# One VectorE and one ScalarE queue reordered around the first output chunk, and one transpose round moved inside a unit

## The chip, the cores and the metric

One core of one Trainium2 chip. The metric is device microseconds of one execution. The kernel before took 497.25 us, the median of 3 runs (497.24 to 497.35).

## The reference

One layer of a model that mixes two kinds of attention, for 256 tokens of width 2048, in float32:

```
h    = rmsnorm(x, g_norm)
proj = h @ w_in                       # 2048 -> 7704 columns: q, k, v, z of both kinds, gates
y_moba = rmsnorm(moba_attention(rope(m_q), rope(m_k), m_v) * silu(m_z), g_out_moba)
y_nsa  = rmsnorm(nsa_attention(rope(n_q), n_q, compressed, selected and window k, v, gates)
                 * silu(n_z), g_out_nsa)
x    = x + concatenate([y_moba, y_nsa]) @ w_out
out  = rmsnorm(x, g_final)
```

The compressed keys of the second kind come from a small two-layer network (`w_ck1`, `w_ck2` and, for the values, `w_cv1`, `w_cv2`), and its raw queries meet these compressed keys without rotation.

## The kernel before

Tokens are two row blocks of 128 (`m` = 0, 1). The input projection is cut into 15 column chunks of 512 (`CHUNKS`), the output projection into 4 more (chunks 15 to 18, `NC` = 15, called output chunk 0 to 3). A **unit** is the part of a chunk that comes from 512 rows of the weight (4 blocks of 128). Units are numbered in the order in which their weights are loaded. Four of them are spoken of often:

- unit 54 is group 1 of output chunk 1 (`UNIT_NO[NC + 1, 1]`)
- units 55, 56 and 57 are groups 1, 2 and 3 of output chunk 0 (`UNIT_NO[NC, 1]` and so on)

To keep float32 precision each operand is split in a rounded part and a residual (`w_hi`, `w_lo`, `xT_hi`, `xT_lo`), and each product is three matmuls (`three_products`, L754 to L756): hi by hi, lo by hi, hi by lo. A unit is 2 row blocks x 4 blocks x 3 = 24 matmuls of 128x512. Its weights go this way:

- SP loads 1 MB into one of three `w_raw` buffers. The load of unit u waits until VectorE has split unit u - 3 (L514).
- ScalarE rounds it into `w_hi` (`hi`, L1189). It waits for the load, and for the ring of three `w_hi`/`w_lo` slots: `unit_used` must count the user of the slot three places back.
- VectorE writes the residual into `w_lo` (`lo`, L1567).
- TensorE waits for `lo_ready` and multiplies.

Five pairs of chunks (`PAIRS`) compute four of their blocks by seven products in place of eight (P1 to P7, `seven`). The pair of output chunks 0 and 1 is called `OA`. It has its own order: `oa_first` (P1, P5, then unit 54), `oa_second` (P2, P6, row block 0 of unit 55, P7, P3), `oa_third` (row block 1 of unit 55, P4). Its weight blocks are rounded by ScalarE (`block_hi`, L1257) and VectorE (`block_lo`, L1850); four intermediate results are copied out of PSUM by ScalarE (`mid_out_`, L1273) and added to the result by DMAs that GpSimd issues (L719). Row block 1 of unit 55 waits for the fourth copy.

The attention result `y` is scaled (`y_scale`), transposed on TensorE (`y_round_`, L735, eight rounds numbered 0 to 7), multiplied by its gain on VectorE (`y_times_g`, L1897), rounded by ScalarE (`y_hi`, L1402) and its residual taken by VectorE (`y_residual`, L1907). Rounds 0 to 3 are the first half of `y`; rounds 4 and 5 are read by unit 56 (`ylo_done` at 6), rounds 6 and 7 by unit 57 (`ylo_done` at 8). `ys` is a combination of parts of `y` for P5 and others, rounded by `ys_round` (L1244) and `ys_residual` (L1824). The last gate chunk z is evacuated by `scaled` on VectorE (L1783), goes through Silu on ScalarE (L1288) and is multiplied into `xo` by GpSimd (L703).

Time is laid out in **slots**. Every engine runs the same loop over slots, and in each slot the `if` lines say which helper is called and in which order. There is no scheduler: what stands first in this code is first in the engine's queue, and a wait in it holds all that stands behind it. `ROUNDED_AT` says in which slot which unit is rounded. `OA_SLOT` is 60, so slots 60 to 62 hold `oa_first` to `oa_third`, slot 63 unit 56 and slot 64 unit 57. `ROUNDS` says after which slots projected rows are transposed on TensorE (`round_`). Round 16 and round 17 transpose the two row blocks of the first four raw queries of the gated (NSA) attention; ScalarE copies each out of the one bank `b_t` into `Q` (`round_out`, L1315) and issues two DMAs from it. Slot 17 runs unit 16. After it, in slot 18, TensorE runs the second layer of the compression network (L997) and the scores of the compressed keys (`cmp_scores`, L1046), which wait for both rounds' copies.

Of the kernel before, what the change touches and what calls it, by code (L numbers as in the profile page):

```python
# [47 lines left out]
NC = len(CHUNKS)  # L48
# [64 lines left out]
UNIT_NO = {u: n for n, u in enumerate(UNITS)}  # L113
# [11 lines left out]
def unit_at(slot):  # L125

    for p, (a, b) in enumerate(X_PAIRS):
        s0 = MIDDLE[p]
        if s0 <= slot < s0 + 2 * UPC:
            return {2: UNIT_NO[a, 2], 3: UNIT_NO[a, 3], 4: UNIT_NO[b, 1], 5: UNIT_NO[b, 2], 7: UNIT_NO[b, 3]}.get(slot - s0)  # L130
    a, b = PAIRS[OUT_PAIR]
    late = LATE[OUT_PAIR]
    if slot >= MIDDLE[OUT_PAIR]:
        return {late + 1: UNIT_NO[a, 2], late + 2: UNIT_NO[a, 3], late + 3: UNIT_NO[b, 1]}.get(slot)
    if slot >= OA_SLOT:
        return UNIT_NO[NC + OUT_UNITS[slot - OA_SLOT - 3][0], OUT_UNITS[slot - OA_SLOT - 3][1]] if slot > OA_SLOT + 2 else None
    return UNIT_NO[slot // UPC, slot % UPC]
# [2 lines left out]

ROUNDED_AT = {9: 10, 10: 11, 11: 12, 12: 13, 13: 14, 14: 15, 15: 16, 17: 17,
              41: 40, 42: 41, 43: 42, 44: 43, 45: 44, 46: 45, 47: 46, 49: 47, 50: 48, 52: 49, 53: 50, 54: 51, 55: 52, 56: 53,
              62: 56, 63: 58, 65: 59, 66: 60, 67: 61, 68: 62, 69: 63, 70: 64, 71: 65}


def rounded_at(slot):
# [42 lines left out]
Q_RAW, Q_MQ, Q_MK = 0, [8, 0], [12, 4]  # L189
Q_COS, Q_SIN = 8, 9  # L190
TRIG_SLOT = 14

def transpose_rounds():
    out = {}
    for i, (kind, _, n) in enumerate(CHUNKS):
# [7 lines left out]
        elif kind in ("mq", "mk"):  # L205
            out[s], out[s + 1] = (kind, (n, 0), i), (kind, (n, 1), i)
    out[TRIG_SLOT] = ("trig", 0, 0)
    return out


ROUNDS = transpose_rounds()
# [83 lines left out]
def build_layer(nc, x, positions, inv_freq, w_in, g_norm, pe_ck, pe_cv, w_ck1, w_ck2, w_cv1, w_cv2,  # L295
# [4 lines left out]
    with ExitStack() as ctx:  # L300
# [431 lines left out]
        def _(pe):  # L732
# [72 lines left out]
                    last = first_product(u, kind, m, k)  # L805
                last.then_inc(unit_used, 1)

            def unit(u):
                if u < UPC:
                    return first_unit(u)  # L810
                c, g = UNITS[u]
                if c >= NC:
                    pe.wait_ge(ylo_done, 4 if g < 2 else 2 * g + 2)
                if g == 0:
                    bank_free(c)
                if u == UPC:
                    pe.wait_ge(xg_early, 2 * UK)
                pe.wait_ge(lo_ready, u - FIRST + 1)
                for m in range(MT):
                    for k in range(UK):  # L820
                        last = three_products(*operands(u, m, k), g == 0 and k == 0, g == UPC - 1 and k == UK - 1, c in PAIR_OF)
                last.then_inc(unit_used, 1)
# [309 lines left out]
            for slot in range(LAST):  # L1132
                for p in range(len(PAIRS)):
                    if slot == EARLY[p] and p != OUT_PAIR:
                        pair_early(p)
                    if slot == MIDDLE[p]:
                        pair_middle(p)
                    if slot == LATE[p]:
                        pair_late(p)
                if slot == OA_SLOT:  # L1140
                    oa_first()
                if slot == OA_SLOT + 1:
                    oa_second()
                if slot == OA_SLOT + 2:
                    oa_third()
                if unit_at(slot) is not None:
                    unit(unit_at(slot))
                if slot == EARLY[OUT_PAIR]:
                    pair_early(OUT_PAIR)
                if slot == 2:  # L1150
                    pe.wait_ge(crow_in, 64)
                    pe.wait_ge(xg_early, 2 * UK)
                    nc.tensor.transpose(b_s[:, 0:P], crows, ident[:, :]).then_inc(crows_T, 1)
                if slot in ROUNDS:
                    round_(slot)
                for c in range(8):
                    if CK_SLOT[c] == slot:
                        ck_unit(c)
                if slot in CK_SUM_SLOT:
                    ck_quarters(CK_SUM_SLOT.index(slot))  # L1160
                if slot in CK2_SLOT:
                    ck_layer2(CK2_SLOT.index(slot))
                if slot in CMP_TOKEN_SLOT:
                    cmp_token(CMP_TOKEN_SLOT.index(slot))
                if slot in CMP_T_SLOT:
                    cmp_T(CMP_T_SLOT.index(slot))
                if slot in CMP_SCORE_SLOT:
                    cmp_scores(CMP_SCORE_SLOT.index(slot))
                if slot == GATE_SLOT:
                    gates()  # L1170
                if slot == GATE_SLOT + 1:
                    gate_quarters()
                if slot - 3 in JOB_AT and ends_head(JOB_AT[slot - 3]):
                    values(JOB_AT[slot - 3])
                if slot - 2 in JOB_AT:
                    prob_T(JOB_AT[slot - 2])
                if slot in JOB_AT:
                    scores(JOB_AT[slot])
                for r in Y_ROUNDS.get(slot, []):
                    y_round_(r)  # L1180
# [3 lines left out]
        def _(act):  # L1184
# [74 lines left out]
            def mid_out_(p, i):  # L1259

                if i == 1:
                    act.wait_ge(unit_used, RING_NO["early", p] + 1)
                else:
                    act.wait_ge(mid_done, 3 * p + (1, 0, 2, 3)[i])
                if p == Z1 and i == 0:
                    act.wait_ge(t_round, len(ROUNDS))
                if p == Z2 and i == 0:
                    act.wait_ge(pv_done, 2 * NH)
                if p == Z2 and i in (1, 2):
                    act.wait_ge(y_done, 2)  # L1270
                if p == OA:
                    act.wait_ge(y_done, 6)
                    nc.scalar.activation(mid_copy(p, i), mid_bank(p, i)[:, :], ACT.Copy, scale=-1.0 if i else 1.0).then_inc(mid_out, 1)  # L1273
                    return
                if p == OUT_PAIR:
                    act.wait_ge(y_done, 8)
                    act.wait_ge(oa_added, 64)
                    nc.scalar.activation(mid_copy(p, i), mid_bank(p, i)[:, :], ACT.Copy).then_inc(mid_out, 1)
                    return
                m = (0, 1, 0, 1)[i]  # L1280
                nc.scalar.activation(mid_copy(p, i), mid_bank(p, i)[:, :], ACT.Copy, scale=rstd[:, m:m + 1]).then_inc(mid_out, 1)
# [143 lines left out]
            for slot in range(NSLOT):  # L1425
# [11 lines left out]
                if slot == OA_SLOT:  # L1437
                    block_hi(OA, 3)
                    y_hi(Y_ROUNDS[57][0])
                    mid_out_(OA, 0)  # L1440
                    mid_out_(OA, 1)
                    hi(UNIT_NO[NC, 1])
                    y_squares(3)
                    block_hi(OA, 4)
                    block_hi(OA, 5)
                    mid_out_(OA, 2)
                if slot == OA_SLOT + 1:
                    mid_out_(OA, 3)
                    block_hi(OA, 6)
# [105 lines left out]
        def _(dve):  # L1555
# [8 lines left out]
            def lo(u):  # L1564
                dve.wait_ge(hi_ready, u - FIRST + 1)
                wh, wl = split_of(u)
                nc.vector.tensor_tensor(wl, w_raw[:, u % RAW], wh.bitcast(F32), ALU.subtract).then_inc(lo_ready, 1)  # L1567
# [254 lines left out]
            def ys_residual():  # L1822
                dve.wait_ge(xs_hi_ok, 3)
                nc.vector.tensor_tensor(ys_lo, ys, ys_hi.bitcast(F32), ALU.subtract).then_inc(xs_lo_ok, 1)  # L1824
# [22 lines left out]
            def block_lo(p, n):  # L1847
                dve.wait_ge(blk_hi, 7 * p + n + 1)
                hi_, lo_ = block_split(p, n)
                nc.vector.tensor_tensor(lo_, block_raw(p, n), hi_.bitcast(F32), ALU.subtract).then_inc(blk_lo, 1)  # L1850
# [20 lines left out]
            def y_scale(half):  # L1871
                dve.wait_ge(rstdy_ok, half + 1)
                for m in range(MT):
                    y = xo[:, m, half * HW:(half + 1) * HW]
                    nc.vector.tensor_scalar(y, y, rstdy[:, half, m:m + 1], None, ALU.mult).then_inc(y_scaled, 1)
# [100 lines left out]
            for slot in range(NSLOT):  # L1976
# [14 lines left out]
                if slot in (8, 40):  # L1991
                    xs_residual((8, 40).index(slot))
                if slot == 57:
                    ys_residual()
                    block_lo(OA, 0)
                    block_lo(OA, 1)
                if slot == OA_SLOT:
                    lo(UNIT_NO[NC + 1, 1])
                    y_parts(Y_ROUNDS[57])
                    block_lo(OA, 2)  # L2000
                    block_lo(OA, 3)
                    lo(UNIT_NO[NC, 1])
                    block_lo(OA, 4)
                    block_lo(OA, 5)
                    y_scale(1)
                if slot == OA_SLOT + 1:
                    block_lo(OA, 6)
                for p in range(len(PAIRS)):
# [119 lines left out]
```

## Time and profile before

| what | value |
|---|---|
| median of 3 runs | 497.25 us |
| the profiled execution, by the device's clock | 497.4 us |
| its span (first to last instruction) | 495.6 us |
| granted TensorE clock, mean over the span | 0.996 of full speed |
| TensorE matmul busy | 484.2 us, 98% of the span |
| VectorE busy | 357.7 us, 72% |
| ScalarE busy | 267.0 us, 54% |
| GpSimd busy | 76.0 us, 15% |
| DMA | 102.22 MB, mean 206 GB/s |

The profiled execution took 497.4 us for a span of 495.6 us; the 1.8 us between them lie before and after the recorded instructions. In a timeline a row is one instruction, or several merged: its start, its length, engine, line, operation, output and inputs, a count, and in brackets how long the engine had been idle before it and what released it. Matmuls overlap: one of 128x512 is recorded with 0.39 us, but the next starts 0.23 us after it, so the distance from start to start is what a matmul costs.

### The profile page before, as it was taken

To read this page: it belongs to the slowest core of one execution; us is meant where nothing else is said; L and a number is where in the kernel's file an instruction comes from. 1 tells how busy PE (TensorE), PEld (TensorE's weight loads), DVE (VectorE), ACT (ScalarE), POOL (GpSimd) and SP (SyncE) were. 2 spreads that over 40 slices of the span, in tenths; PEclk is the share of its full clock that TensorE was granted. 3 is DMA by queue.
4 is the path that set the end of the run, shared out by engine and by line. 5 is a ranking of instruction groups with operands and counts; after the bars stand their busy time and mean duration, and the time that the engine had idled before them with its cause. 6 is when DMAs were issued, how large, how long until landed. Compare 5 with 4: busy or idle time off the path is not lost.

```text
span 495.6 us, 6581 instructions
## 1 busy us (share of the span) xinstructions
PE 484.2 (98%) x2508; PEld 401.6 (81%) x2508; DVE 357.7 (72%) x568; ACT 267.0 (54%) x383; POOL 76.0 (15%) x75
## 2 busy tenths in 40 slices
PE   8999999999999999999999999999999999899994
PEld 7887787777788888888888888888888887688883
DVE  5888855932799948766587878765877787988644
ACT  5886353632656535544544464665665675466422
POOL 2340100100102202000020200000534236040220
PEclk9999999999999999999999999999999999999998
DMA  8989894577476452543443734446699948973404
GB/s 291 335 278 385 300 327 154 186 264 250 138 261 192 171 171 85 171 154 106 166 167 131 255 93 147 145 162 263 216 293 304 291 170 233 310 265 104 149 1 169
DMA packets 59311, 102.22 MB, mean 206 GB/s; under 512 B 4784, under 2 KB 15632, under 8 KB 58896
## 3 DMA queue, kind: packets, MB, share of 16 engines
q1 hardware_dynamic: 55136, 97.08, 56.6%
q0 software_dynamic: 1936, 3.67, 4.2%
q10 hardware_dynamic: 2208, 1.06, 0.9%
q8 instruction: 20, 0.33, 0.3%
q14 instruction: 11, 0.09, 0.0%
HBM read 97.60 MB, written 2.10 MB: 201 GB/s over the span
## 4 chain that ended last, share of the span: by engine, by line
PE 91%; DVE 3%; issue 2%; ACT 2%; DMA 1%; ACTq 0%; POOLq 0%; POOL 0%; SPq 0%; DVEq 0%
PE proj L754 25%; PE proj L756 24%; PE proj L755 24%; PE b_o L1103 4%; PE b_t L735 2%; PE b_p L1072 2%; PE proj L787 2%; PE b_s L973 2%; PE proj L798 1%; PE proj L793 1%; DVE w_lo L1567 1%; DMA w_raw<-in_w_in_dram 1%; ACT w_hi L1189 1%; PE b_s L756 1%; PE b_s L754 1%
## 5 line engine op out<-in xcount | busy, mean ns | idle before, releaser
L754 PE MATMUL proj<-w_hi,xT_hi 128*128 128x512 f32 (+1 forms) x498 | 195.8, 393 | 2.1 <-DVE w_lo L1567 2.1
L756 PE MATMUL proj<-w_hi,xT_lo 128*128 128x512 f32 (+1 forms) x498 | 193.8, 389 | 0.0
L755 PE MATMUL proj<-w_lo,xT_hi 128*128 128x512 f32 (+1 forms) x498 | 193.6, 389 | 0.0
L1567 DVE TENSOR_TENSOR w_lo<-w_raw,w_hi 128x2048 fp32r<-128x2048 f32 x63 | 145.0, 2304 | 60.4 <-ACT w_hi L1189 60.3
L1189 ACT ACTIVATE w_hi<-w_raw 128x2048 fp32r<-128x2048 f32 x63 | 120.3, 1913 | 30.2 <-PE proj L756 18.1
L754 PEld LDWEIGHTS proj<-w_hi,xT_hi 128*128 128x128 f32 x498 | 93.5, 188 | 23.1 <-issue 4.2
L756 PEld LDWEIGHTS proj<-w_hi,xT_lo 128*128 128x128 f32 x498 | 93.5, 188 | 19.9
L755 PEld LDWEIGHTS proj<-w_lo,xT_hi 128*128 128x128 f32 x498 | 93.6, 188 | 18.3
L694 POOL TENSOR_TENSOR rope_a<-rope_a,rope_b 128x512 f32<-128x512 f32 (+1 forms) x12 | 15.0, 1274 | 165.4 <-DVE rope_b L1654 165.4
L1347 ACT ACTIVATE pT<-b_p 128x512 f32<-128x512 f32 (+2 forms) x24 | 11.8, 490 | 51.4 <-PE b_p L1072 51.4
L1850 DVE TENSOR_TENSOR w_lo<-blk_b,w_hi 128x1024 fp32r<-128x1024 f32 x17 | 21.0, 1234 | 17.3 <-ACT w_hi L1257 17.3
L1257 ACT ACTIVATE w_hi<-blk_b 128x1024 fp32r<-128x1024 f32 x17 | 17.9, 1054 | 16.6 <-DVE blk_b L1858 12.6
L1341 ACT ACTIVATE prob<-prob,nmx 128x256 f32<-128x256 f32 (+1 forms) x48 | 21.3, 447 | 6.8 <-DVE nmx L1750 6.8
L754 PE MATMUL proj<-w_hi,ymT_hi 128*128 128x512 f32 x60 | 23.7, 396 | 0.3 <-DVE w_lo L1567 0.3
L756 PE MATMUL proj<-w_hi,ymT_lo 128*128 128x512 f32 x60 | 23.4, 390 | 0.0
L755 PE MATMUL proj<-w_lo,ymT_hi 128*128 128x512 f32 x60 | 23.4, 390 | 0.0
L1746 DVE CUSTOM_DVE_ANT_0 prob<-b_s,mask 128x256 f32<-128x256 f32 (+1 forms) x48 | 15.1, 353 | 8.1 <-PE b_s L756 8.1
L724 POOL TENSOR_TENSOR Q<-Q,KV 128x512 f32<-128x512 f32 x6 | 10.5, 1774 | 49.2 <-ACT rope_c L1408 49.2
L703 POOL TENSOR_TENSOR xo<-xo,rope_a 128x512 f32<-128x512 f32 x4 | 7.6, 1931 | 67.8 <-DVE xo L1770 63.7
L681 POOL TENSOR_TENSOR rope_a<-rope_a,rope_b 128x512 f32<-128x512 f32 x4 | 5.6, 1394 | 60.9 <-DVE rope_b L1667 60.9
L1770 DVE COPY xo<-b_o 128x256 f32<-128x256 f32 x16 | 6.7, 420 | 10.6 <-PE b_o L1103 10.6
L1315 ACT ACTIVATE Q<-b_t 128x512 f32<-128x512 f32 x9 | 5.3, 593 | 15.8 <-PE b_t L735 15.7
(287 smaller groups left out, 621.5 us busy)
## 6 DMA issues: line engine op xcount, KB each, us to landing
w_raw<-in_w_in_dram SPq DMA_DIRECT2D x51, 1024.0 KB, 5.1
w_raw<-in_w_out_dram SPq DMA_DIRECT2D x12, 1024.0 KB, 5.7
xo<-in_w_ck_dram SPq DMA_DIRECT2D x4, 1024.0 KB, 8.3
xo<-in_w_cv_dram SPq DMA_DIRECT2D x4, 1024.0 KB, 7.2
w_raw<-in_w_in_dram SPq DMA_DIRECT2D x12, 256.0 KB, 6.1
Q<-in_x_dram SPq DMA_DIRECT2D x2, 1024.0 KB, 7.1
out_dram<-Q SPq DMA_DIRECT2D x8, 256.0 KB, 2.7
xo<-in_x_dram SPq DMA_DIRECT2D x3, 512.0 KB, 7.2
```

Source lines behind the costliest of these rows:

```text
L694: nc.gpsimd.tensor_tensor(rope_a[:, m, 0:w], rope_a[:, m, 0:w], rope_b[:, m, 0:w], ALU.add).then_inc(rope_sum, 1)
L754: nc.tensor.matmul(dst, a_hi, b_hi, start=first, stop=False, skip_group_check=goes_on)
L755: nc.tensor.matmul(dst, a_hi, b_lo, start=False, stop=False, skip_group_check=goes_on)
L756: return nc.tensor.matmul(dst, a_lo, b_hi, start=False, stop=last, skip_group_check=goes_on)
L1103: last = nc.tensor.matmul(b_o[:, m * P:(m + 1) * P], a, v, start=n == 0, stop=n == len(prods) - 1)
L1189: nc.scalar.activation(split_of(u)[0], w_raw[:, u % RAW], ACT.Copy).then_inc(hi_ready, 1)
L1257: nc.scalar.activation(block_split(p, n)[0], block_raw(p, n), ACT.Copy).then_inc(blk_hi, 1)
L1341: last = nc.scalar.activation(prob[:, b, c0:c1], prob[:, b, c0:c1], ACT.Exp, bias=nmx[:, b, n:n + 1], scale=SCALE, accum_out=sums[:, b, n: ...
L1347: nc.scalar.activation(pT[:, j % 2, 0:width(j)], b_p[:, 0:width(j)], ACT.Copy).then_inc(pt_out, 1)
L1567: nc.vector.tensor_tensor(wl, w_raw[:, u % RAW], wh.bitcast(F32), ALU.subtract).then_inc(lo_ready, 1)
L1746: nc.vector.tensor_tensor_reduce(out=prob[:, j % 2, c0:c1], in0=b_s[:, c0:c1], in1=mask[:, slice(*mask_cols(j, n))], scale=1.0, scalar=NEG ...
L1850: nc.vector.tensor_tensor(lo_, block_raw(p, n), hi_.bitcast(F32), ALU.subtract).then_inc(blk_lo, 1)
```

## The change

Four moves of calls within the slot code. No instruction is added or removed, and no operand changes.

- ScalarE rounds unit 56 in slot 60, between the third and the fourth PSUM copy of `OA`. Before, it did so in slot 62, behind the rounding of transposed `y` rounds 4 and 5.
- VectorE takes the residual of unit 56 in slot 60 behind `y_scale(1)`. Before, it did so in slot 62, behind rounds 4 and 5 of `y`.
- VectorE takes in slot 57 first the residuals of the two first `OA` blocks, then that of `ys`, then that of unit 54, and only then evacuates z. Before, the residual of `ys` stood first, and that of unit 54 stood behind z.
- TensorE runs transpose round 17 between the two row blocks of unit 16, and not behind the unit.

```diff
--- before.py
+++ after.py
@@ -140,7 +140,7 @@
 
 ROUNDED_AT = {9: 10, 10: 11, 11: 12, 12: 13, 13: 14, 14: 15, 15: 16, 17: 17,
               41: 40, 42: 41, 43: 42, 44: 43, 45: 44, 46: 45, 47: 46, 49: 47, 50: 48, 52: 49, 53: 50, 54: 51, 55: 52, 56: 53,
-              62: 56, 63: 58, 65: 59, 66: 60, 67: 61, 68: 62, 69: 63, 70: 64, 71: 65}
+              63: 58, 65: 59, 66: 60, 67: 61, 68: 62, 69: 63, 70: 64, 71: 65}
 
 
 def rounded_at(slot):
@@ -189,6 +189,7 @@
 Q_RAW, Q_MQ, Q_MK = 0, [8, 0], [12, 4]
 Q_COS, Q_SIN = 8, 9
 TRIG_SLOT = 14
+INNER_ROUND = 17
 
 
 
@@ -805,7 +806,8 @@
                     last = first_product(u, kind, m, k)
                 last.then_inc(unit_used, 1)
 
-            def unit(u):
+            def unit(u, between=None):
+
                 if u < UPC:
                     return first_unit(u)
                 c, g = UNITS[u]
@@ -817,6 +819,8 @@
                     pe.wait_ge(xg_early, 2 * UK)
                 pe.wait_ge(lo_ready, u - FIRST + 1)
                 for m in range(MT):
+                    if m and between is not None:
+                        round_(between)
                     for k in range(UK):
                         last = three_products(*operands(u, m, k), g == 0 and k == 0, g == UPC - 1 and k == UK - 1, c in PAIR_OF)
                 last.then_inc(unit_used, 1)
@@ -1144,14 +1148,14 @@
                 if slot == OA_SLOT + 2:
                     oa_third()
                 if unit_at(slot) is not None:
-                    unit(unit_at(slot))
+                    unit(unit_at(slot), slot if slot == INNER_ROUND else None)
                 if slot == EARLY[OUT_PAIR]:
                     pair_early(OUT_PAIR)
                 if slot == 2:
                     pe.wait_ge(crow_in, 64)
                     pe.wait_ge(xg_early, 2 * UK)
                     nc.tensor.transpose(b_s[:, 0:P], crows, ident[:, :]).then_inc(crows_T, 1)
-                if slot in ROUNDS:
+                if slot in ROUNDS and slot != INNER_ROUND:
                     round_(slot)
                 for c in range(8):
                     if CK_SLOT[c] == slot:
@@ -1444,6 +1448,7 @@
                     block_hi(OA, 4)
                     block_hi(OA, 5)
                     mid_out_(OA, 2)
+                    hi(UNIT_NO[NC, 2])
                 if slot == OA_SLOT + 1:
                     mid_out_(OA, 3)
                     block_hi(OA, 6)
@@ -1991,11 +1996,11 @@
                 if slot in (8, 40):
                     xs_residual((8, 40).index(slot))
                 if slot == 57:
-                    ys_residual()
                     block_lo(OA, 0)
                     block_lo(OA, 1)
+                    ys_residual()
+                    lo(UNIT_NO[NC + 1, 1])
                 if slot == OA_SLOT:
-                    lo(UNIT_NO[NC + 1, 1])
                     y_parts(Y_ROUNDS[57])
                     block_lo(OA, 2)
                     block_lo(OA, 3)
@@ -2003,6 +2008,7 @@
                     block_lo(OA, 4)
                     block_lo(OA, 5)
                     y_scale(1)
+                    lo(UNIT_NO[NC, 2])
                 if slot == OA_SLOT + 1:
                     block_lo(OA, 6)
                 for p in range(len(PAIRS)):
```

On TensorE the move is one of place alone: in slot 17 the four transposes `b_t<-ident,raw_e` stood behind the 24 matmuls of unit 16 and directly ahead of L997 and L1046; now they stand behind the first 12, and 12 matmuls lie between them and L997 (L1001 in the changed file; L1046 is L1050). The three other moves are shown below.

VectorE, slots 57 and 60. L1824 (now L1829) is the residual of `ys`, L1850 (L1855) that of an `OA` block, L1783 (L1788) the evacuation of z, L1567 (L1572) the residual of a whole unit: here of unit 54. Before:

```order
L1824 TENSOR_TENSOR xT_lo<-raw_e,xT_hi 128x1024
L1850 TENSOR_TENSOR w_lo<-Q,w_hi 128x1024 x2
L1783 SCALAR_TENSOR_TENSOR rope_b<-proj,rstd,KV 128x512 x2
L1567 TENSOR_TENSOR w_lo<-w_raw,w_hi 128x2048
L1897 TENSOR_TENSOR pT<-b_o,ccols 128x512
L1907 TENSOR_TENSOR ymT_lo<-pT,ymT_hi 128x4x128
```

The change:

```order
L1855 TENSOR_TENSOR w_lo<-Q,w_hi 128x1024 x2
L1829 TENSOR_TENSOR xT_lo<-raw_e,xT_hi 128x1024
L1572 TENSOR_TENSOR w_lo<-w_raw,w_hi 128x2048
L1788 SCALAR_TENSOR_TENSOR rope_b<-proj,rstd,KV 128x512 x2
L1902 TENSOR_TENSOR pT<-b_o,ccols 128x512
L1912 TENSOR_TENSOR ymT_lo<-pT,ymT_hi 128x4x128
```

The residual of unit 54 has gone ahead of z and stands directly behind three residuals.

ScalarE, slots 60 to 62. L1273 (now L1277) with output `prob` are the third and fourth copies of `OA`, L1257 (L1261) with `KV` the last `OA` block, L1402 (L1406) the rounding of `y`, L1189 (L1193) the rounding of a unit. Before:

```order
L1273 ACTIVATE prob<-proj 128x512 x2
L1257 ACTIVATE w_hi<-KV 128x1024
L1402 ACTIVATE xT_hi<-pT 128x4x128 x2
L1189 ACTIVATE w_hi<-w_raw 128x2048
L1402 ACTIVATE xT_hi<-pT 128x4x128 x2
L1189 ACTIVATE w_hi<-w_raw 128x2048 x2
```

The change:

```order
L1277 ACTIVATE prob<-proj 128x512
L1193 ACTIVATE w_hi<-w_raw 128x2048
L1277 ACTIVATE prob<-proj 128x512
L1261 ACTIVATE w_hi<-KV 128x1024
L1406 ACTIVATE xT_hi<-pT 128x4x128 x4
L1193 ACTIVATE w_hi<-w_raw 128x2048 x2
```

The rounding of unit 56 has left its place between `y` rounds 4, 5 and 6, 7 for the one between the two copies. VectorE's residual of unit 56 goes the same way: from behind L1907 of rounds 4 and 5 to directly behind L1880, `y_scale(1)`. Before:

```order
L1875 TENSOR_SCALAR xo<-xo,rstdy 128x1024 x2
L1850 TENSOR_TENSOR w_lo<-KV,w_hi 128x1024
L1897 TENSOR_TENSOR pT<-b_t,ccols 128x512
L1897 TENSOR_TENSOR pT<-b_s,ccols 128x512
L1907 TENSOR_TENSOR xT_lo<-pT,xT_hi 128x4x128 x2
L1567 TENSOR_TENSOR w_lo<-w_raw,w_hi 128x2048
L1897 TENSOR_TENSOR pT<-b_p,ccols 128x512
```

The change:

```order
L1880 TENSOR_SCALAR xo<-xo,rstdy 128x1024 x2
L1572 TENSOR_TENSOR w_lo<-w_raw,w_hi 128x2048
L1855 TENSOR_TENSOR w_lo<-KV,w_hi 128x1024
L1902 TENSOR_TENSOR pT<-b_t,ccols 128x512
L1902 TENSOR_TENSOR pT<-b_s,ccols 128x512
L1912 TENSOR_TENSOR xT_lo<-pT,xT_hi 128x4x128 x2
L1902 TENSOR_TENSOR pT<-b_p,ccols 128x512
```

It now stands ahead of the residual of the last `OA` block, which P4 waits for.

## Rows read from the trace of the kernel before

**Rows 1.** The page, busy time of each engine.

```profile
PE 484.2 (98%) x2508; PEld 401.6 (81%) x2508; DVE 357.7 (72%) x568; ACT 267.0 (54%) x383; POOL 76.0 (15%) x75
```

**Rows 2.** Waits of PE: us in total, times, longest us.

```profile
PE proj L754 <- DVE w_lo L1567: 2.4, 3, 1.8
```

**Rows 3.** Timeline of PE around its three waits; start us, us, instruction, idle before.

```profile
409.62 0.39 PE L756 MATMUL proj<-w_hi,xT_lo 128*128 128x512 f32 x1
410.33 0.47 PE L754 MATMUL proj<-w_hi,ymT_hi 128*128 128x512 f32 x1 [0.33 <-DVE w_lo L1567]
...
416.33 0.60 PE L735 MATMUL b_s<-ident,xo 128*128 128x128 f32 x4
416.68 0.48 PE L754 MATMUL proj<-w_hi,ymT_hi 128*128 128x512 f32 x1
...
421.32 0.60 PE L735 MATMUL b_o<-ident,xo 128*128 128x128 f32 x4
423.67 0.47 PE L754 MATMUL proj<-w_hi,xT_hi 128*128 128x512 f32 x1 [1.76 <-DVE w_lo L1567]
...
428.98 0.39 PE L756 MATMUL proj<-w_hi,xT_lo 128*128 128x512 f32 x1
429.67 0.47 PE L754 MATMUL proj<-w_hi,xT_hi 128*128 128x512 f32 x1 [0.30 <-DVE w_lo L1567]
```

**Rows 4.** Timeline of DVE, slots 57 to 62.

```profile
394.35 1.22 DVE L1824 TENSOR_TENSOR xT_lo<-raw_e,xT_hi 128x1024 fp32r<-128x1024 f32 x1 [2.17 <-ACT xT_hi L1244]
...
399.13 1.41 DVE L1783 SCALAR_TENSOR_TENSOR rope_b<-proj,rstd,KV 128x512 f32<-128x512 f32 x2 [1.28 <-PE proj L756]
400.46 2.28 DVE L1567 TENSOR_TENSOR w_lo<-w_raw,w_hi 128x2048 fp32r<-128x2048 f32 x1
...
404.04 1.67 DVE L1907 TENSOR_TENSOR ymT_lo<-pT,ymT_hi 128x512 fp32r<-128x512 f32 x1 [0.70 <-ACT ymT_hi L1402]
...
407.90 2.28 DVE L1567 TENSOR_TENSOR w_lo<-w_raw,w_hi 128x2048 fp32r<-128x2048 f32 x1
...
416.31 1.23 DVE L1850 TENSOR_TENSOR w_lo<-KV,w_hi 128x1024 fp32r<-128x1024 f32 x1 [1.82 <-ACT w_hi L1257]
...
418.83 1.29 DVE L1907 TENSOR_TENSOR xT_lo<-pT,xT_hi 128x512 fp32r<-128x512 f32 x2
...
423.44 0.68 DVE L1897 TENSOR_TENSOR pT<-b_p,ccols 128x512 f32<-128x512 f32 x1
```

**Rows 5.** Timeline of ACT, slots 57 to 62.

```profile
394.23 1.91 ACT L1189 ACTIVATE w_hi<-w_raw 128x2048 fp32r<-128x2048 f32 x1
...
403.38 0.63 ACT L1402 ACTIVATE ymT_hi<-pT 128x512 fp32r<-128x512 f32 x1 [0.86 <-DVE pT L1897]
...
414.73 0.60 ACT L1273 ACTIVATE prob<-proj 128x512 f32<-128x512 f32 x1 [4.09 <-PE proj L756]
...
419.30 1.90 ACT L1189 ACTIVATE w_hi<-w_raw 128x2048 fp32r<-128x2048 f32 x1
```

**Rows 6.** Timeline of POOL: the first product of z and y, and two issued DMAs.

```profile
401.13 2.77 POOL L703 TENSOR_TENSOR xo<-xo,rope_b 128x512 f32<-128x512 f32 x1 [12.40 <-ACT rope_b L1288]
...
414.59 2.02 POOL L719 DMA_DIRECT2D Q<-prob  x2
```

**Rows 7.** POOL L703 with `rope_b`, all four: duration ns min/median/max, first and last start.

```profile
L703 POOL TENSOR_TENSOR xo<-xo,rope_b x4: 1296/1846/2767, 366.9 to 403.9; 128x512 f32<-128x512 f32 x4
```

**Rows 8.** Timeline of SP: two loads of units, the second waited for.

```profile
402.77 7.81 SPq L514 DMA_DIRECT2D w_raw<-in_w_out_dram  x2
```

**Rows 9.** Timeline of PE around slot 18.

```profile
127.80 0.65 PE L997 MATMUL b_o<-prob,hidT 128*32 128x128 f32 x16
128.56 0.64 PE L1046 MATMUL b_p<-Q,kcT 128*32 128x256 f32 x8
```

**Rows 10.** Timeline of ACT, the copies of rounds 16 and 17.

```profile
121.54 0.60 ACT L1315 ACTIVATE Q<-b_t 128x512 f32<-128x512 f32 x1 [5.69 <-PE b_t L735]
...
127.91 0.60 ACT L1315 ACTIVATE Q<-b_t 128x512 f32<-128x512 f32 x1 [2.25 <-PE b_t L735]
```

## The prediction, made before the changed kernel had run

> **What bounds the kernel now.** I read first the page. TensorE is busy for 484.2 of 495.6 us and no other engine passes 72% [rows 1], so a gain can only come from the few places where TensorE stands still. The table of waits names them: three waits for the residual of a unit's weights, 2.4 us together [rows 2]. Only then did I ask the timeline for their places. TensorE's starts jump at 410.33 (unit 55), at 423.67 (unit 56) and at 429.67 (unit 57), each time released by L1567 of VectorE [rows 3]. These are the units of output chunk 0, and they are the ones that the change moves. The table has only these three for L1567 and nothing else behind them, so from 429.67 to the last matmul TensorE never waits, so what is won there should arrive whole at the end. A fourth, smaller stop is at 128.56: the scores of the compressed keys start 0.05 us after ScalarE's copy of round 17 has ended at 128.51 [rows 9, 10].
>
> What a stop costs is more than its bracket, since matmuls overlap. The distance between starts is 0.71 us at 410.33, where 0.23 is normal; the start after that one comes 0.31 later, so 0.08 more is lost: **0.56 us** in all. Behind four transposes the next matmul normally starts 0.35 us later (416.33 to 416.68); at 423.67 it is 2.35: **2.00 us**. At 429.67 it is 0.69 in place of 0.23: 0.46, with the slow restart 0.54 [rows 3].
>
> **Part 1: VectorE in slot 57.** VectorE was idle for 2.17 us before 394.35, and the two block residuals that it then took had long had their input. In front of them, they run from 392.2 to 394.5; the residual of `ys` follows to 395.7, in place of 395.6 [rows 4]. ScalarE has rounded unit 54 by 396.14 [rows 5], so its residual runs from 396.2 to 398.4, in the idle time ahead of z at 399.13 (1.28 us idle there) [rows 4]. Cost nothing; z, whose input comes from TensorE, starts where it did. What VectorE saves behind z is 2.2 us: `y` round 3 is multiplied at 400.5, not 402.7. ScalarE has to end a block first (it is free at 402.52, the 0.86 us idle ahead of 403.38) [rows 5], so it rounds round 3 from 402.5 to 403.15, and VectorE takes its residual from 403.2, not 404.04 [rows 4].
>
> How long that residual takes is unknown. In the trace it took 1.67 us where its neighbours take 0.68 (1.29 for two) [rows 4], and GpSimd was multiplying z into `xo` beside it: its first product took 2.77 us, the shortest of its kind 1.30, and the second began at 403.9 [rows 6, 7]. The residual of unit 54 ran until 402.74, in the first part of that 2.77. With the worst reading the residual of round 3 ends where it did, at 405.71, and nothing is won for unit 55. With 1.67 again it ends at 404.9. With 0.68 behind products of 1.3 us each, which would start at 401.13 and end at 403.7, it ends at 404.4. Two block residuals (2.3 us) and the residual of unit 55 (2.28) follow: 406.7, then 409.0 for the last value, 409.5 for the middle one. TensorE wants unit 55 at 409.85. So in both, unit 55's stop of 0.56 us goes; I take that, and keep 0 for the range. The rule that bears on it: the Trainium skill, page "SBUF — State Buffer", section "SBUF: two separate sides", says that a VectorE instruction with two SBUF inputs and a GpSimd instruction that reads SBUF lock each other out for a whole instruction. The trace agrees (GpSimd's first product could only run behind 402.74, and 1.2 us later it is done; the residual at 404.04 ends 0.55 us behind GpSimd's end). By this rule the stop of unit 55 goes with 0.9 us to spare; if the long residual had another cause that stays, the forecast would be 0.56 us higher.
>
> **Part 2: unit 56.** ScalarE was idle for 4.09 us before it made the fourth copy at 414.73 [rows 5]. The ring slot that unit 56 needs is free when row block 0 of unit 55 is through: 12 matmuls of 0.23 us from 409.8, so 412.6. The rounding takes 1.9 us, to 414.5; the fourth copy then runs to 415.15, the last `OA` block to 416.2 (the copy ended at 415.33 before [rows 5]). VectorE takes the residual of unit 56 from 414.6 to 416.9. Unit 56 wants it at 423.67 - 0.56 - 2.00 = 421.11. So the stop of 2.00 us goes, with 4 us to spare.
>
> What pays for it is queued behind. On ScalarE: row block 1 of unit 55 waits for the fourth copy, which comes at 415.15, and starts at 416.68 - 0.56 = 416.1: 0.9 us to spare. On VectorE: the last block's residual goes from 416.31 [rows 4] to 416.9 and ends at 418.1; P4 wants it 12 matmuls behind 416.1, at 418.8: 0.7 to spare. Rounds 4 and 5 follow. From that block's start to the end of their residuals it was 420.12 - 416.31 = 3.81 us [rows 4], so now 420.7, against 421.11: 0.4 us to spare, the tightest of all. I count 0 for each, up to 1 us in the range.
>
> **Part 3: unit 57.** With unit 56 out of the way round 6 of `y` is multiplied as soon as it is transposed and VectorE is free, near 420.95, not at 423.44 [rows 4]. From there to TensorE's restart at 429.67 it was 6.23 us [rows 3, 4]: rounding, residuals, rounding and residual of unit 57, all in a row, and none of it changes. So TensorE restarts at 427.18. It would be ready at 421.11 + 5.54 = 426.65: the third stop stays, 0.53 us in place of 0.46. From here the whole program runs 429.67 - 427.18 = **2.49 us** earlier. Loads move along or more: SP's load of unit 57 went out at 402.77, when the residual of unit 54 was done [rows 8], and goes out near 398.4 now.
>
> **Part 4: round 17 inside unit 16.** TensorE does the same work. The bank is free: ScalarE had copied round 16 by 122.14 [rows 10], and the new place is 12 matmuls, 2.8 us, ahead of the old, so near 124.5, as L997 behind the old one starts at 127.80 [rows 9]. The copy of round 17, ended at 128.51 before, is then made some 2 us sooner, and the scores no longer wait for it. The network before them is recorded until 128.45, the scores start at 128.56 [rows 9]: **0.1 us** won. Entering and leaving transposes costs once more inside a unit and once less behind it, so nothing either way; I keep 0.1 loss to 0.2 gain.
>
> The sum is 2.49 + 0.1 = 2.6 us. The profiled execution took 497.4 us, 0.15 over the median shown: 494.8 against it, and 494.65 against the median. I forecast 494.7.
>
> **The rivals.** (a) *A small new wait takes over at unit 56 or 55*: the residual of round 3 stays as late as it was, or rounds 4 and 5 miss their 0.4 us because VectorE's residual of unit 56 stands ahead of them. For: the thin margin, and two DMAs that GpSimd issues at 414.59 for 2.02 us [rows 6], just where VectorE now has instructions with two SBUF inputs. Against: before, the block residual at 416.31 ran beside their end in its usual 1.23 us [rows 4, 6]. Price 0.56 to 1.2 us: 495.2 to 495.8. (b) *The gain is given back behind 430*, where weights' loads would set the pace: against it stands that no wait is left there, and that every load is released by a residual that itself comes 2.5 us or more earlier. It would give 497.0 to 497.3. (c) *Slower*: VectorE's queue slips. The residual of unit 56 waits in front of the last block and of rounds 4 and 5; if ScalarE's rounding of it were held, by the ring slot or by GpSimd's issues, P4 and unit 56 would wait for all of it. Beyond 0.4 us each us costs one, so it ends slower when VectorE is 3 us late there. At 4 us late, two issues of 2.02 [rows 6], the time is 494.7 + 3.6 = 498.3. Against it: unit 56's weights were loaded far earlier, and only one DMA issue is left once the fourth copy is made. (d) *The change doesn't do what it says*: the order of the queues shows all four moves, so I give it nothing of its own.
>
> **How the numbers follow.** Forecast 0.77, (a) 0.14, (b) 0.05, (c) 0.04. The range: below, the third stop goes too (0.5 us), 494.1; above it takes in (a) to 495.8. A measurement of this kernel can tell 0.2%, 1.0 us. The forecast and (a) lie below 496.25, with a little left for a bad sum of both: faster 0.91; (b) and the rest within 0.2%: 0.05; slower 0.04.
>
> **What would show it.** Right: TensorE's waits for L1567 fall from three to one, of about 0.3 us in its bracket, in front of unit 57; unit 55 starts near 409.8 and unit 57 near 427.2, both less the 0.1 of part 4; the residual of round 3 takes about 0.7 us, and GpSimd's two products 1.3 each. Wrong: a wait in front of row block 1 of unit 55 (ScalarE's copy), of P4 (L1850's counterpart) or of unit 56 (L1907's), or new waits behind 430.

## The result and the profile after

The changed kernel took 494.51 us (median of 4 runs, 494.39 to 494.64), the kernel before 497.29 (497.24 to 497.35): 2.78 us less, a ratio of 0.9944 with a 95% interval of 0.9927 to 0.9961. The forecast was 494.7.

| what | before | after |
|---|---|---|
| median, us | 497.29 | 494.51 |
| span of the profiled execution, us | 495.6 | 492.7 |
| TensorE matmul busy, us | 484.2 | 483.7 |
| TensorE's waits for L1567 (now L1572) | 3, 2.4 us | 1, 0.4 us |
| granted TensorE clock, mean | 0.996 | 0.997 |

The work is the same on every engine and so is the clock; what went is time in which TensorE stood still. The waits of TensorE in the changed kernel (us in total, times, longest), against [rows 2]:

```profile
PE proj L755 <- DVE w_lo L1572: 0.4, 1, 0.4
```

Of the three stops of [rows 3] one is left. TensorE's timeline after, at the places of the three: the start of unit 55, the start of unit 56 behind the transposes, and the start of unit 57.

```profile
409.23 0.39 PE L757 MATMUL proj<-w_hi,xT_lo 128*128 128x512 f32 x1
409.46 0.39 PE L755 MATMUL proj<-w_hi,ymT_hi 128*128 128x512 f32 x1
...
420.33 0.60 PE L736 MATMUL b_o<-ident,xo 128*128 128x128 f32 x4
420.68 0.48 PE L755 MATMUL proj<-w_hi,xT_hi 128*128 128x512 f32 x1
...
425.99 0.39 PE L757 MATMUL proj<-w_hi,xT_lo 128*128 128x512 f32 x1
426.76 0.47 PE L755 MATMUL proj<-w_hi,xT_hi 128*128 128x512 f32 x1 [0.38 <-DVE w_lo L1572]
```

From start to start it is now 0.23 us at unit 55 (0.71 before), 0.35 at unit 56 (2.35) and 0.77 at unit 57 (0.69). Unit 57 starts 2.91 us earlier than it did, and that stays to the end: the span is 2.9 shorter.

VectorE's queue after, against [rows 4]:

```profile
391.76 2.35 DVE L1855 TENSOR_TENSOR w_lo<-Q,w_hi 128x1024 fp32r<-128x1024 f32 x2
394.03 1.22 DVE L1829 TENSOR_TENSOR xT_lo<-raw_e,xT_hi 128x1024 fp32r<-128x1024 f32 x1
395.81 2.29 DVE L1572 TENSOR_TENSOR w_lo<-w_raw,w_hi 128x2048 fp32r<-128x2048 f32 x1 [0.57 <-ACT w_hi L1193]
398.78 1.41 DVE L1788 SCALAR_TENSOR_TENSOR rope_b<-proj,rstd,KV 128x512 f32<-128x512 f32 x2 [0.68 <-PE proj L757]
...
402.72 1.17 DVE L1912 TENSOR_TENSOR ymT_lo<-pT,ymT_hi 128x512 fp32r<-128x512 f32 x1 [1.93 <-ACT ymT_hi L1406]
...
406.09 2.28 DVE L1572 TENSOR_TENSOR w_lo<-w_raw,w_hi 128x2048 fp32r<-128x2048 f32 x1
...
414.39 2.29 DVE L1572 TENSOR_TENSOR w_lo<-w_raw,w_hi 128x2048 fp32r<-128x2048 f32 x1 [1.72 <-ACT w_hi L1193]
416.60 1.22 DVE L1855 TENSOR_TENSOR w_lo<-KV,w_hi 128x1024 fp32r<-128x1024 f32 x1
...
419.12 1.29 DVE L1912 TENSOR_TENSOR xT_lo<-pT,xT_hi 128x512 fp32r<-128x512 f32 x2
420.53 0.69 DVE L1902 TENSOR_TENSOR pT<-b_p,ccols 128x512 f32<-128x512 f32 x1
```

The two block residuals, that of `ys` and that of unit 54 fill the time ahead of z, which still waits for TensorE (0.68 us of idle time are left there). Unit 55's residual ends at 408.37, 1.1 us ahead of unit 55's start at 409.46. Unit 56's ends at 416.68, and behind it rounds 4 and 5 end at 420.41, 0.27 us ahead of unit 56's start. And z's product on GpSimd, against [rows 6, 7], two of them one behind the other:

```profile
400.79 2.55 POOL L704 TENSOR_TENSOR xo<-xo,rope_b 128x512 f32<-128x512 f32 x2 [12.63 <-ACT rope_b L1292]
```

ScalarE's copies and unit 56's rounding, against [rows 5]:

```profile
409.66 0.60 ACT L1277 ACTIVATE prob<-proj 128x512 f32<-128x512 f32 x1 [0.65 <-PE proj L757]
412.44 1.92 ACT L1193 ACTIVATE w_hi<-w_raw 128x2048 fp32r<-128x2048 f32 x1 [2.18 <-PE proj L757]
414.26 0.57 ACT L1277 ACTIVATE prob<-proj 128x512 f32<-128x512 f32 x1
414.74 1.05 ACT L1261 ACTIVATE w_hi<-KV 128x1024 fp32r<-128x1024 f32 x1
```

The fourth copy ends at 414.83, 0.9 us ahead of the row block of unit 55 that waits for it. The last block's residual ends at 417.82, 0.7 us ahead of P4. These two starts on TensorE are:

```profile
415.69 0.48 PE L755 MATMUL proj<-w_hi,ymT_hi 128*128 128x512 f32 x1
...
418.53 0.39 PE L755 MATMUL proj<-w_hi,ymT_hi 128*128 128x512 f32 x1
```

### The profile page after: what moved, and what is told of

The parts are those of the page before. It is cut to its first block, busy times and chain, and to the rows that moved or that the text cites. A ratio compares the mean times of both kernels' runs of the same rounds, so it can differ in the third digit from the quotient of the medians.

```text
span 492.7 us, 6581 instructions
## 1 busy us (share of the span) xinstructions
PE 483.7 (98%) x2508; PEld 401.9 (82%) x2508; DVE 358.3 (73%) x568; ACT 267.0 (54%) x383; POOL 74.1 (15%) x75
## 4 chain that ended last, share of the span: by engine, by line
PE 95%; issue 1%; DVE 1%; DMA 1%; ACT 1%; ACTq 0%; POOLq 0%; POOL 0%; SPq 0%; DVEq 0%
PE proj L755 25%; PE proj L757 25%; PE proj L756 25%; PE b_o L1107 4%; PE b_t L736 2%; PE b_p L1076 2%; PE proj L788 2%; PE b_s L977 2%; PE proj L794 1%; PE proj L799 1%; PE proj L894 1%; DMA w_raw<-in_w_in_dram 1%; PE b_s L757 1%; PE b_s L755 1%; PE b_s L756 1%
## 5 line engine op out<-in xcount | busy, mean ns | idle before, releaser
L1572 DVE TENSOR_TENSOR w_lo<-w_raw,w_hi 128x2048 fp32r<-128x2048 f32 x63 | 145.7, 2316 | 59.6 <-ACT w_hi L1193 59.4
L1193 ACT ACTIVATE w_hi<-w_raw 128x2048 fp32r<-128x2048 f32 x63 | 120.4, 1913 | 31.8 <-PE proj L757 20.6
L1855 DVE TENSOR_TENSOR w_lo<-blk_b,w_hi 128x1024 fp32r<-128x1024 f32 x17 | 21.0, 1234 | 17.4 <-ACT w_hi L1261 17.4
L1261 ACT ACTIVATE w_hi<-blk_b 128x1024 fp32r<-128x1024 f32 x17 | 17.9, 1055 | 16.5 <-DVE blk_b L1863 12.6
L1768 DVE TENSOR_SCALAR prob<-prob,coef 128x256 f32<-128x256 f32 (+1 forms) x48 | 13.2, 317 | 0.9
```

Of the source, the lines that this page charges most:

```text
L1193: nc.scalar.activation(split_of(u)[0], w_raw[:, u % RAW], ACT.Copy).then_inc(hi_ready, 1)
L1261: nc.scalar.activation(block_split(p, n)[0], block_raw(p, n), ACT.Copy).then_inc(blk_hi, 1)
L1768: last = nc.vector.tensor_scalar(prob[:, j % 2, c0:c1], prob[:, j % 2, c0:c1], coef[:, j % 2, i:i + 1], None, ALU.mult)
```

## The experiments

### Each part alone

Three kernels each carry one part of the change on top of the kernel before.

Part 1, VectorE's slot 57:

```diff
                 if slot == 57:
-                    ys_residual()
                     block_lo(OA, 0)
                     block_lo(OA, 1)
+                    ys_residual()
+                    lo(UNIT_NO[NC + 1, 1])
                 if slot == OA_SLOT:
-                    lo(UNIT_NO[NC + 1, 1])
```

> Only VectorE's order in slot 57 is changed, nothing else. My theory (the parts are separate, each stop has its own cause): the residual of unit 54 ends near 398.5 us, unit 55's stop at 410.33 goes, the stops at units 56 and 57 stay at their size (2.35 and 0.69 from start to start), so 0.56 us are won and the time is 496.7. Rival (the later chain through ScalarE's rounding of unit 56 does not move along, since it hangs on something else): the wait at unit 56 grows by what unit 55 gave up, and the time stays at 497.2 to 497.3.

Measured: 496.70 us (496.55 to 496.90, 10 runs) beside 497.37 for the kernel before on the same chip (19 runs, 497.20 to 497.62 and one of 499.32), ratio 0.9982 (0.9973 to 0.9992). 0.67 us are won, and by the interval anything from 0.4 to 1.3 would fit. TensorE's waits for a unit's residual:

```profile
PE proj L754 <- DVE w_lo L1567: 2.1, 2, 1.8
```

Two are left, at units 56 and 57, as long as they were (1.76 and 0.31 us in their brackets). The stop of unit 55 has its own cause, and the chain behind it moves along. It was worth a little more than the 0.56 us that I read: the matmuls after a restart keep a slightly longer distance (2.16 us for the nine from 410.33 to 412.49 in the trace before, where nine at 0.227 are 2.04), and I had counted only the first of them. That makes 0.60; the rest is less than the runs differ among themselves. Part 1 is two moves, the block residuals ahead of that of `ys` and the residual of unit 54 ahead of z, and no run has one without the other.

Part 2, unit 56:

```diff
-              62: 56, 63: 58, 65: 59,
+              63: 58, 65: 59,
...
                     mid_out_(OA, 2)
+                    hi(UNIT_NO[NC, 2])
...
                     y_scale(1)
+                    lo(UNIT_NO[NC, 2])
```

> Only the rounding and the residual of unit 56 go to slot 60; slot 57 and round 17 are as before. My theory: unit 55's stop of 0.71 from start to start stays, the stop of 2.00 us at unit 56 goes, that of unit 57 stays: 1.9 to 2.0 us won, the time is 495.3 to 495.4. Round 3's residual keeps its 1.67 us. Rival (part 2 needs the slack that part 1 gives, as VectorE's queue is too late for P4 or for rounds 4 and 5): a new wait of 0.5 us or more at P4 or unit 56, and 495.8 or more.

Measured: 495.37 us (495.32 to 495.44, 4 runs), ratio 0.9959 (0.9944 to 0.9974). 2.00 us are won. TensorE waits in front of units 55 and 57 and no longer in front of unit 56:

```profile
410.18 0.47 PE L754 MATMUL proj<-w_hi,ymT_hi 128*128 128x512 f32 x1 [0.34 <-DVE w_lo L1568]
...
427.60 0.47 PE L754 MATMUL proj<-w_hi,xT_hi 128*128 128x512 f32 x1 [0.38 <-DVE w_lo L1568]
```

Round 3's residual keeps its length, as its surroundings are those of before:

```profile
403.88 1.67 DVE L1908 TENSOR_TENSOR ymT_lo<-pT,ymT_hi 128x512 fp32r<-128x512 f32 x1 [0.70 <-ACT ymT_hi L1402]
```

So part 2 needs nothing from part 1. The room for rounds 4 and 5 of `y` can be read here too. Their residuals end at 421.25, and unit 56 starts at 421.52, 0.27 us later:

```profile
419.96 1.29 DVE L1908 TENSOR_TENSOR xT_lo<-pT,xT_hi 128x512 fp32r<-128x512 f32 x2
...
421.52 0.48 PE L754 MATMUL proj<-w_hi,xT_hi 128*128 128x512 f32 x1
```

Part 4, round 17:

```diff
                 for m in range(MT):
+                    if m and between is not None:
+                        round_(between)
                     for k in range(UK):
...
-                    unit(unit_at(slot))
+                    unit(unit_at(slot), slot if slot == 17 else None)
...
-                if slot in ROUNDS:
+                if slot in ROUNDS and slot != 17:
                     round_(slot)
```

> Only transpose round 17 goes between the row blocks of unit 16. My theory after the changed kernel's trace: 0.3 us won, all of it as a shorter distance from the network's start to the scores' start (0.76 to 0.46 us), and everything behind it 0.3 earlier to the end: 497.0. Rival (the 0.3 is eaten by one of the three later stops, since they wait for VectorE and not for TensorE): the first stop at 410.33 grows by 0.3 and the time stays at 497.3.

Measured: 497.01 us (496.84 to 497.11, 10 runs), ratio 0.9992 (0.9983 to 1.0002). The interval touches 1, so the time alone doesn't settle it; the medians lie 0.36 us apart, and the timeline shows the place. Here are the network and the scores in this kernel, against [rows 9]:

```profile
127.68 0.64 PE L999 MATMUL b_o<-prob,hidT 128*32 128x128 f32 x16
128.15 0.61 PE L1048 MATMUL b_p<-Q,kcT 128*32 128x256 f32 x8
```

The scores start 0.47 us behind the network's start, not 0.76. At unit 57 TensorE starts at 429.19 in place of 429.67, and the brackets of the three stops are unchanged, so nothing of it is eaten on the way (some 0.1 us of the 0.48 lies ahead of slot 16 in this execution).

The three alone make 0.67 + 2.00 + 0.36 = 3.03 us. All together they gave 2.78 in the first comparison and 2.85 in the repeat further down (497.37 to 494.52): they add up, within the 0.1 to 0.3 us between the runs of one kernel and the 0.08 by which unit 57's stop has grown.

### What held the residual of round 3

The kernel before, with GpSimd multiplying only a quarter of the columns of the last z chunk into `xo`. It leaves out three quarters of that product, so its output is another, and only its times are of use.

```diff
                     for m in range(MT):
                         pool.wait_ge(z_ok, 2 * n + m + 1)
-                        nc.gpsimd.tensor_tensor(xo[:, m, n * CW:(n + 1) * CW], xo[:, m, n * CW:(n + 1) * CW],
-                                                z[:, m, :], ALU.mult).then_inc(y_done, 1)
+                        w = CW // 4 if n == 3 else CW
+                        nc.gpsimd.tensor_tensor(xo[:, m, n * CW:n * CW + w], xo[:, m, n * CW:n * CW + w],
+                                                z[:, m, 0:w], ALU.mult).then_inc(y_done, 1)
```

> The kernel before, but GpSimd multiplies only a quarter of the columns (128 of 512) of the last z chunk into xo, so three quarters of that chunk's product are left out and the output is another. VectorE's and ScalarE's queues are those of before. Lock theory (a VectorE instruction with two SBUF inputs and a GpSimd product keep each other out): GpSimd is done before VectorE's residual of y round 3 starts at 404.04, so that residual takes 0.68 us in place of 1.67, unit 55's stop goes, and about 0.56 us are won. Rival (the long residual has another cause, such as ScalarE's copies or the DMA beside it): it keeps 1.6 us or so and the time stays at 497.3.

Measured: 496.69 us, one run, beside 497.43 for the kernel before. VectorE and GpSimd at the place, a timeline of each:

```profile
403.93 0.69 DVE L1908 TENSOR_TENSOR ymT_lo<-pT,ymT_hi 128x512 fp32r<-128x512 f32 x1 [0.70 <-ACT ymT_hi L1403]
```

```profile
401.02 2.35 POOL L704 TENSOR_TENSOR xo<-xo,rope_b 128x128 f32<-128x128 f32 x2 [13.06 <-ACT rope_b L1289]
```

GpSimd is done at 403.37, and the residual, with its queue and its start as before, takes 0.69 us in place of 1.67. TensorE's waits for a unit's residual are two, not three:

```profile
PE proj L755 <- DVE w_lo L1568: 2.1, 2, 1.8
```

The stop of unit 55 is gone, and the 0.74 us of this one run agree with the 0.67 of part 1 alone. GpSimd's product was what held VectorE. The three readings fit one rule: before, the residual started at 404.04 with GpSimd busy to 405.16, and took 1.67; in the changed kernel it started at 402.72 with GpSimd busy to 403.34, and took 1.17; here GpSimd was through, and it took 0.69. In the first two it ended 0.55 us behind GpSimd, though they had run beside each other for 1.12 us in one and 0.62 us in the other. So VectorE got nothing done while GpSimd ran: two engines that only slowed each other would have left less after the longer overlap. The two products before, for the 405.16:

```profile
401.13 4.03 POOL L703 TENSOR_TENSOR xo<-xo,rope_b 128x512 f32<-128x512 f32 x2 [12.40 <-ACT rope_b L1288]
```

That is the exclusive port of the Trainium skill, page "SBUF — State Buffer", section "SBUF: two separate sides": of a VectorE instruction with two SBUF inputs and a GpSimd one that reads SBUF, the later waits for all of the earlier. The first product's 2.77 us in [rows 6] fit it as well: the residual of unit 54 ran until 402.74, and the product ended 1.16 us behind it, a little less than the 1.30 of an undisturbed one. In the changed kernel that residual is over before GpSimd starts, and both products take 2.55 together.

### How tight VectorE's queue is

The changed kernel, with half of unit 56's residual (128x1024) taken once more ahead of the whole. `late_step` is a semaphore of its own for the step from the first to the second.

```diff
+                if twice:
+                    nc.vector.tensor_tensor(wl[:, 0:2], w_raw[:, u % RAW, 0:2], wh[:, 0:2].bitcast(F32), ALU.subtract).then_inc(late_step, 1)
+                    dve.wait_ge(late_step, 1)
                 nc.vector.tensor_tensor(wl, w_raw[:, u % RAW], wh.bitcast(F32), ALU.subtract).then_inc(lo_ready, 1)
```

`twice` is set for unit 56 alone.

> The changed kernel with 1.2 us more work on VectorE behind y_scale: half of unit 56's residual is taken twice. Theory (rounds 4 and 5 of y have only 0.27 us to spare at unit 56 in the changed kernel, P4 some 0.7, and each us beyond costs one): unit 56 starts 0.9 to 1.0 us later, the chain to unit 57 1.1 later, and the time is 495.5 to 495.7. Rival (VectorE has room there, the margin is larger than it looks, since waits are polled or rows merged): 494.5 to 494.8.

Measured: 495.56 us (495.46 to 495.78, 5 runs), ratio to the kernel before 0.9963 (0.9949 to 0.9977): 1.04 us more than the changed kernel on the same chip (494.52, below). VectorE's added instruction and the whole residual behind it:

```profile
414.39 1.23 DVE L1574 TENSOR_TENSOR w_lo<-w_raw,w_hi 128x1024 fp32r<-128x1024 f32 x1 [1.72 <-ACT w_hi L1194]
415.65 2.29 DVE L1576 TENSOR_TENSOR w_lo<-w_raw,w_hi 128x2048 fp32r<-128x2048 f32 x1
```

TensorE at P4 and at unit 56:

```profile
418.31 0.39 PE L758 MATMUL proj<-w_hi,ymT_lo 128*128 128x512 f32 x1
419.14 0.50 PE L756 MATMUL proj<-w_hi,ymT_hi 128*128 128x512 f32 x1 [0.45 <-DVE w_lo L1859]
...
421.07 0.60 PE L737 MATMUL b_o<-ident,xo 128*128 128x128 f32 x4
421.73 0.50 PE L756 MATMUL proj<-w_hi,xT_hi 128*128 128x512 f32 x1
```

P4 now waits (0.83 us from start to start), unit 56 waits again for rounds 4 and 5 (0.66 behind the transposes, not 0.35) and starts 1.05 us later than in the changed kernel. Of 1.26 us more on VectorE (from 414.39 to 415.65) 1.05 reach unit 56; 0.2 was the room. The margin that I had called the tightest is real, and it is small.

### The stop that is left, and a faster kernel

In the changed kernel unit 57 waits for a chain of steps: VectorE's product of rounds 6 and 7, ScalarE's rounding of both, ScalarE's rounding of unit 57, VectorE's residual of it. The rounding of the unit needs none of `y`, and ScalarE is idle ahead of round 6. So it goes first:

```diff
+                if slot == 62:
+                    hi(UNIT_NO[NC, 3])
                 for r in Y_ROUNDS.get(slot, []):
                     if slot != 57:
                         y_hi(r)
-                if slot == 62:
-                    hi(UNIT_NO[NC, 3])
```

> The changed kernel, and on ScalarE in slot 62 the rounding of unit 57 ahead of that of y rounds 6 and 7. My theory (the stop left at unit 57 is the row of VectorE product, ScalarE roundings, VectorE residuals, rounding, residual of 6.23 us, of which the rounding of 1.9 us can lie in ScalarE's idle time before round 6): ScalarE rounds unit 57 from 419.7 to 421.6, its residual ends near 425.9, TensorE wants it at 426.22, so the last stop goes and 0.6 us are won: 493.9. Rival (the ring slot of unit 57 is free only later, or rounds 6 and 7 then come too late): the stop stays or turns into a wait for y's residuals, 494.4 to 495.

Measured: 493.84 us (493.73 to 494.12, 4 runs), ratio 0.9929 (0.9912 to 0.9945). ScalarE and VectorE there:

```profile
419.64 1.90 ACT L1193 ACTIVATE w_hi<-w_raw 128x2048 fp32r<-128x2048 f32 x1
421.44 1.14 ACT L1406 ACTIVATE xT_hi<-pT 128x512 fp32r<-128x512 f32 x2
```

```profile
422.09 1.29 DVE L1912 TENSOR_TENSOR xT_lo<-pT,xT_hi 128x512 fp32r<-128x512 f32 x2 [0.22 <-ACT xT_hi L1406]
423.30 4.49 DVE L1572 TENSOR_TENSOR w_lo<-w_raw,w_hi 128x2048 fp32r<-128x2048 f32 x2
```

The rounding of rounds 6 and 7 is 0.2 us later, the residual of unit 57 begins at 423.30 and not at 424.32. TensorE's starts run on at 0.23 us through 425.6 to 427, and the list of its waits names no `w_lo` any more.

As the step is small, both kernels ran again beside each other on one chip.

> The changed kernel unaltered, beside the one with unit 57 rounded first, on one chip: 494.4 to 494.6.

> The changed kernel with unit 57 rounded ahead of y rounds 6 and 7, measured again beside it: 0.6 us below the changed kernel, 493.8 to 493.9. Rival (the first measurement was luck): no difference that the runs' spread of 0.2 us lets one see.

Measured: the changed kernel 494.52 (494.46 to 494.72, 5 runs), with unit 57 rounded first 493.82 (493.74 to 494.02, 5 runs). The runs don't overlap: 0.70 us, 0.14% of the time. Against the kernel before the second is at 0.993 (0.9917 to 0.9943).

Does that last step need the change before it?

```diff
-                    hi(UNIT_NO[NC, 2])
...
-                    lo(UNIT_NO[NC, 2])
...
-              63: 58, 65: 59,
+              62: 56, 63: 58, 65: 59,
```

on top of the kernel with unit 57 rounded first.

> As the one before, but unit 56 is rounded in slot 62 as in the kernel before. Theory (every stop has its own cause and price): the stop of 2.0 us at unit 56 is back, that of unit 57 stays away: 495.8 to 495.9. Rival (unit 57's stop is only gone because unit 56 came early): both are back, 496.4.

Measured: 495.75 us (495.69 to 495.96, 5 runs), ratio 0.9969 (0.9956 to 0.9981). TensorE's only wait for a unit's residual in this kernel:

```profile
422.51 0.47 PE L755 MATMUL proj<-w_hi,xT_hi 128*128 128x512 f32 x1 [1.76 <-DVE w_lo L1571]
```

Unit 56's stop is back in full, unit 57's stays away. The two stops have each a cause and a price of their own.

## Why the prediction was right

- **The bound.** That the gain could only be TensorE's standing time, and that it would arrive whole at the end, held: 2.91 us at unit 57, 2.9 in the span. Rival (b), a gain given back behind 430, didn't happen in any run.
- **Part 1.** The order of events came as worked out. The residual of unit 54 ends at 398.1 (said: 398.4), with the whole trace 0.35 us earlier by then. The residual of round 3 ended at 403.89 (said: 404.4, or 404.05 with those 0.35). The stop of unit 55 went, for some 0.6 us where I had 0.56. That GpSimd's products would delay the residual of round 3 was one of three readings in the prediction, named with its rule; the quarter product has since shown it. Only my last paragraph was careless: it asked for a residual of 0.7 us there, while the working above it had the residual held to GpSimd's end, and 1.17 is what that gives.
- **Part 2.** 2.00 us said, 2.00 measured alone. The fourth copy had 0.9 us to spare and P4 0.7, both as said. The margin for rounds 4 and 5 was 0.27 us, not 0.4. It isn't that TensorE came sooner: ScalarE's rounding of unit 56 is released by row block 0 of unit 55, so all the steps behind it move with TensorE, and part 2 alone, with unit 55 still late and round 17 in its old place, has the same 0.27. The steps took 0.1 us more than I had sized them: 10.95 us from unit 55's start to the end of those residuals, where 420.7 - 409.85 makes 10.85. The largest miss is the first step. I let the ring slot come free 12 starts behind unit 55's start, 2.75 us, and ScalarE started 2.98 us behind it (409.46 to 412.44), as the twelfth matmul started at 411.95 but is recorded until 412.34. With a few tenths less, rival (a) would have begun; the kernel with 1.26 us more on VectorE shows its price, nearly one for one beyond the margin.
- **Part 3.** The chain of 6.23 us from round 6's product to TensorE's restart was 6.23 again (420.53 to 426.76). The stop stayed, 0.77 from start to start (said: 0.76).
- **Part 4.** This is the term that was mis-sized: 0.1 us said, 0.3 measured. I had taken the network's recorded end, 128.45, for the moment from which the scores could run. Ends of matmuls are modelled and overlap what follows. From start to start the pair needs 0.47 us, and in the trace before it was 0.76: the difference is the wait, 0.3. I had used exactly that reading for the three large stops and not for this one.
- **A misread row.** Rival (c) took its 4 us from "two issues of 2.02". [rows 6] give 2.02 us for the two together, so the price of two held issues there would be 494.7 + 1.6 = 496.3 and not 498.3. In the changed kernel VectorE's residual of unit 56 followed ScalarE's rounding at once (414.36 to 414.39), and no issue held it.

The sum was 2.6 us and 2.8 came by the medians, 2.9 at unit 57 in the two traces. Of the 0.3 between the sum and the traces 0.2 is part 4 and less than 0.1 is unit 55; the rest, again less than 0.1, has no place found.

## What to carry to other kernels

In a kernel whose main engine is busy for 98%, ask for its few waits and price each from start to start against the same pair of instructions elsewhere; the bracket of idle time and the recorded ends undercount it. Then follow the waiting unit's chain backwards through the helper engines and look for a step that needs nothing of what stands ahead of it in the queue, beside an idle time that it would fit into. Check what it is put ahead of with the same care: here 0.27 us of room decided between the whole gain and a part of it. Count it from one common start: where the main engine itself releases the helper's first step, the helper's work moves along when the main engine comes sooner.

## What the runs showed of the hardware

- A VectorE subtraction of two SBUF tiles (128x512) took 0.69, 1.17 or 1.67 us, by how long GpSimd's product was still running when it started; in both of the longer ones it ended 0.55 us behind GpSimd. Its recorded time holds the wait. A move on VectorE thus also sped up GpSimd: its two products took 2.55 us together, and 4.03 before.
- After a wait the second matmul starts 0.31 us behind the first and the next ones at up to 0.24, where 0.23 is normal, so that the stops at units 55 and 57 cost some 0.1 us more than their gap. Behind four transposes it is the same without any wait (0.32 at 420.68 in the changed kernel), so unit 56's stop, which stood behind transposes, cost its gap alone.
- Four 128x128 float32 transposes in the middle of a unit cost what they cost behind it. From unit 16's first matmul to the network's start it was 6.10 us before (121.70 to 127.80) and 6.12 after (121.69 to 127.81).
